# Activations, conditioning, states and small vectors handed over with channels on partitions, in the mLSTM + NSA decoder step

## The reference, cut to what matters

```python
def ada_norm(x, c, g, w_ada, b_ada):
    shift, scale, gate = jnp.split(c @ w_ada + b_ada, 3, axis=-1)
    h = rmsnorm(x, g) * (1 + scale[:, None, :]) + shift[:, None, :]
    return h, gate[:, None, :]

def mlstm_layer(x, c, C0, n0, m0, conv0, norm_g, ada_w, ada_b, w_in, gate_b, conv_w, conv_b, wq, wk, ...):
    h, gate = ada_norm(x, c, norm_g, ada_w, ada_b)
    proj = h @ w_in                     # xc, v, o, z and the gates ig, fg
    ...                                 # short convolution from conv0, q and k by 4x4 blocks wq, wk
    ...                                 # stabilised matrix memory from C0, n0, m0
    return x + gate * out, (C, n, m, new_conv)

def nsa_layer(x, c, ...):
    h, gate = ada_norm(x, c, norm_g, ada_w, ada_b)
    ...
    out = (o.astype(x.dtype) * jax.nn.silu(z)) @ w_out
    return x + gate * out               # y_prompt (1, 512, 1024) and y_sample (8, 4, 1024)
```

## Time and profile before

| what | value |
|---|---|
| median of 3 runs | 2076.85 us (2076.14 to 2081.01) |
| span of the profiled execution | 2075.2 us |
| PE busy | 1912.7 us, 92% of the span |
| DVE, ACT, POOL busy | 712.8, 473.6, 227.0 us |
| moved by DMA | 281.79 MB, mean 136 GB/s |

### The profile page before, as it was taken

One profiled execution on the slowest core, in us unless ns is written; L12 is line 12 of the kernel. 1 busy time (PEld: TensorE's weight loads), 2 busy tenths in 40 slices (PEclk: granted clock), 3 DMA queues, 4 the chain that ended last, 5 costly groups with the idle time before them and its releaser, 6 DMA issues. The chain is left out here.

```text
span 2075.2 us, 26135 instructions
## 1 busy us (share of the span) xinstructions
PE 1912.7 (92%) x9695; PEld 1154.3 (56%) x9695; DVE 712.8 (34%) x1620; ACT 473.6 (23%) x1032; POOL 227.0 (11%) x333
## 2 busy tenths in 40 slices
PE   5779999999999999997989999789889999999878
PEld 3345645564655565456864448655555555555467
DVE  3213232323242423240121314167652444444332
ACT  1311211211131112110011011246442333333310
POOL 0000100010001000100000000024352112111000
PEclk8879999999999999998999999779899999999989
DMA  9942561355135422635121236500024444443431
GB/s 299 387 155 72 201 215 43 120 180 187 43 143 183 162 80 106 229 116 219 41 81 41 81 59 245 169 26 2 1 79 186 177 179 173 182 178 123 138 88 43
DMA packets 119388, 281.79 MB, mean 136 GB/s; under 512 B 33320, under 2 KB 41966, under 8 KB 115543
## 3 DMA queue, kind: packets, MB, share of 16 engines
q1 hardware_dynamic: 101100, 170.57, 24.7%
q0 software_dynamic: 12928, 109.54, 13.2%
q10 hardware_dynamic: 5268, 0.36, 0.3%
HBM read 227.79 MB, written 60.86 MB: 139 GB/s over the span
## 5 line engine op out<-in xcount | busy, mean ns | idle before, releaser
L2187 PE MATMUL sample_bank<-area 128*128 128x508 f32 x512 | 234.3, 600 | 4.8 <-DVE area L2428 4.8
L1080 DVE SCALAR_TENSOR_TENSOR mlstm_cring<-mlstm_cring,mlstm_cur_old,mlstm_bank 128x512 f32<-128x512 f32 x128 | 87.1, 743 | 223.4 <-PE mlstm_bank L842 223.4
L2187 PEld LDWEIGHTS sample_bank<-area 128*128 128x128 f32 x512 | 92.0, 190 | 106.6 <-issue 98.7
L1368 PE MATMUL proj_bank<-stage,area 128*128 128x512 f32 x320 | 142.4, 603 | 6.3 <-ACT area L1445 6.3
L760 PE MATMUL mlstm_bank<-h,stage 128*128 128x272 f32 x512 | 126.7, 411 | 15.4 <-issue 10.9
L760 PEld LDWEIGHTS mlstm_bank<-h,stage 128*128 128x128 f32 x512 | 102.0, 200 | 39.3 <-issue 12.6
L815 PE MATMUL mlstm_bank<-h,stage 128*128 128x272 f32 x512 | 121.2, 395 | 0.0
L826 PE MATMUL mlstm_bank<-stage,h 128*128 128x512 f32 x256 | 114.1, 599 | 0.0
L815 PEld LDWEIGHTS mlstm_bank<-h,stage 128*128 128x128 f32 x512 | 96.0, 190 | 27.9 <-issue 9.1
L777 PE MATMUL mlstm_bank<-stage,h 128*128 128x512 f32 x256 | 110.9, 594 | 0.0
L1368 PEld LDWEIGHTS proj_bank<-stage,area 128*128 128x128 f32 x320 | 60.9, 193 | 87.5 <-issue 85.9
(11 more groups left out here) (513 smaller groups left out, 2709.1 us busy)
## 6 DMA issues: line engine op xcount, KB each, us to landing
stage<-in_a_w_in SPq DMA_DIRECT2D x16, 2048.0 KB, 8.9
mlstm_cring<-in_state_C SPq DMA_DIRECT2D x32, 1024.0 KB, 5.5
o_Cs<-mlstm_cring POOLq DMA_DIRECT2D x32, 1024.0 KB, 4.7
stage<-in_a_ada_w SPq DMA_DIRECT2D x4, 2048.0 KB, 12.6
sample_winr<-in_cache_kv_win SPq DMA_DIRECT2D x8, 1024.0 KB, 5.3
o_win_s<-in_cache_kv_win SPq DMA_DIRECT2D x1, 8128.0 KB
stage<-in_w_kv SPq DMA_DIRECT2D x3, 2048.0 KB, 7.7
act_scratch<-mlstm_szt POOLq DMA_DIRECT2D x4, 1088.0 KB, 8.3
```

Source lines behind the costliest of these rows:

```text
L1080: dve.scalar_tensor_tensor(c, c, cur_old[:, n:n + 1], bank[:, b_big("outer", n * KH + k), :], ALU.mult, ALU.add).then_inc(E["c_new"], 1)
L1368: last = pe.matmul(o, h[:, k, a * P:(a + 1) * P], w[:, k, :], start=(k == 0), stop=(k == KD - 1))
L2187: t = pe.matmul(out, S.w1[:, c, o * 8 + k, :], xt[:, k, :, o:o + M - 1], start=(k == 0 and o == 0), stop=(k == 7 and o == 1))
```

## The change

What arrives in HBM is laid out by the host: `x_t` (128 x 8 x 544, x of prompt and samples with channels on partitions), `first` (the turned conditioning, padded with zeros to 32 columns, and the gate weights, padded to 32), `vec` (the ten vectors with channels on partitions), `heads` (gate biases and `state_m`), `state` (`a_wq`, `a_wk`, the turned state of the convolution and the turned `n0`). 19 inputs go, 5 come. All transposes of L289 to L316 and the DVE copies of L467 to L481 go, and the spill with them; `phase_project` loads `x_t` in place of `S.x_scratch`. The output `y` leaves as 128 x 8 x 544 and the host turns it; each of the 8 blocks of `S.x1` is stored when it is ready.

```diff
@@ phase_inputs
-        x_nat = sb("x_nat", [P, TT, D])
-        xs_nat = sb("xs_nat", [SS, D])
-        c_nat = sb("c_nat", [NS + 1, D])
-        c_t = sb("c_t", [P, KD, SS])
-        rows1 = sb("rows1", [88, P])
-        rows2 = sb("rows2", [112, P])
-        conv_nat = sb("conv_nat", [NS * (CW - 1), AI])
+        first = sb("first", [P, 2, KD, SS])
+        c_t, gate_w = first[:, 0], first[:, 1]
...
@@ SP
             sp.dma_start(S.const1[:, :], I["const"][0:AH, S.n_late:]).then_inc(s_const, 16)
-            sp.dma_start(c_nat[0:1, :], I["c_prompt"]).then_inc(s_c, 16)
-            sp.dma_start(c_nat[1:, :], I["c_sample"]).then_inc(s_c, 16)
...
-            sp.dma_start(x_nat[:, :, :], I["x_prompt"].rearrange("o (a p) d -> p (o a) d", p=P)).then_inc(s_x, 16)
-            sp.dma_start(xs_nat[:, :], I["x_sample"].rearrange("n t d -> (n t) d")).then_inc(s_x, 16)
+            sp.dma_start(flat(first[:, :, :, :], "pgks"), I["first"]).then_inc(s_first, 16)
+            sp.dma_start(xt[:, :, :], I["x_t"]).then_inc(s_x, 16)
...
             for i in range(NCH):
-                if i == 2:
-                    sp.wait_ge(x_ok, KD + 1)
-                    sp.dma_start(S.x_scratch, xt[:, :, :]).then_inc(spill, 16)
                 if uses(i):
                     sp.wait_ge(ada_mm, earlier(i) + 1)
                 elif SLOT[i] == 2:
                     sp.wait_ge(sum_ok, 1)
                 elif SLOT[i] == 3:
-                    sp.wait_ge(spill, 16)
                     sp.wait_ge(x_used, 1)
@@ POOL
-            pool.memset(S.n0[0:1, :], 0.0)
-            pool.memset(m0[:, 0:1], 0.0)
-            pool.memset(gate_w[:, :, :], 0.0)
...
+            pool.memset(S.n0[0:1, :], 0.0).then_inc(zero_ok, 1)
@@ PE
             pe.wait_ge(s_const, 32)
-            pe.wait_ge(s_vec, 160)
...
+            pe.wait_ge(s_first, 16)
@@ ACT
-            act.dma_start(conv_nat[:, :], I["state_conv"].rearrange("o n j c -> (o n j) c")).then_inc(s_conv, 16)
...
+            act.dma_start(S.vec[:, :], I["vec"]).then_inc(s_vec, 16)
+            act.dma_start(heads[:, :], I["heads"]).then_inc(s_m0, 16)
+            act.dma_start(S.state[:, :], I["state"]).then_inc(s_state, 16)
+            act.dma_start(S.n0[1:, :], I["state_n"].rearrange("o n h d -> (o n) (h d)")).then_inc(s_state, 16)
+
+            act.wait_ge(s_x, 16)
             act.activation(sq[:, :, :], xt[:, :, :], ACT.Square).then_inc(sq_ok, 1)
@@ phase_project
-            sp.dma_start(S.x1[:, :, :], S.x_scratch).then_inc(E["x_in"], 16)
+            sp.dma_start(S.x1[:, :, :], I["x_t"]).then_inc(E["x_in"], 16)
@@ phase_output
-            for a in range(TT):
-                sp.wait_ge(E["y_ok"], 2 * a + 2)
-                sp.dma_start(I["o_yp"].rearrange("o (a p) d -> p (o a) d", p=P)[:, a, :], y[:, a, :]).then_inc(E["outs"], 16)
-            sp.wait_ge(E["y_ok"], 10)
-            sp.dma_start(I["o_ys"].rearrange("n t d -> (n t) d"), ys[:, :]).then_inc(E["outs"], 16)
-            sp.wait_ge(E["outs"], 16 * (TT + 1))
+            for m in range(KD):
+                sp.wait_ge(E["x_new"], m + 1)
+                sp.dma_start(I["o_y"][:, m, :], S.x1[:, m, :]).then_inc(E["outs"], 16)
+            sp.wait_ge(E["outs"], 16 * KD)
...
-            pe.wait_ge(E["x_new"], KD)
-
-            for a in range(TT + 1):
...
-                        last = pe.transpose(bank[0:rows, b, k * P:(k + 1) * P], S.x1[:, half * 4 + k, at:at + rows], ident)
-                    last.then_inc(E["tr"], 1)
...
-                dve.tensor_copy(dst, bank[0:rows, f % 8, :]).then_inc(E["y_ok"], 1)
```

More of the change, by code:

```diff
@@ L2585, in _ @@
                 last.then_inc(E["mm"], 1)
-            pe.wait_ge(E["x_new"], KD)
-            for a in range(TT + 1):
-                for half in range(2):
-                    f = 2 * a + half
-                    b = f % 8
-                    if f >= 8:
-                        pe.wait_ge(E["y_ok"], f - 7)
-                    rows, at = (P, a * P) if a < TT else (SS, TP)
-                    for k in range(4):
-                        last = pe.transpose(bank[0:rows, b, k * P:(k + 1) * P], S.x1[:, half * 4 + k, at:at + rows], ident)
-                    last.then_inc(E["tr"], 1)
         @block.vector
@@ L2704, in build, with small_layouts, turned @@
         phase_output(nc, I, S)
+def small_layouts(given):
+    def turned(a, rows):
+        return np.asarray(a).reshape(rows, -1, P).transpose(2, 1, 0)
+    x = np.concatenate([np.asarray(given["x_prompt"]).reshape(TP, D), np.asarray(given["x_sample"]).reshape(SS, D)], 0)
+    first = np.zeros((P, 2, KD, SS), np.float32)
+    first[:, 0, :, 0:1], first[:, 0, :, 1:NS + 1] = turned(given["c_prompt"], 1), turned(given["c_sample"], NS)
+    first[:, 1, :, 0:2 * AH] = np.asarray(given["a_w_in"])[0, :, 4 * AI:].reshape(KD, P, 2 * AH).transpose(1, 0, 2)
+    vec = np.concatenate([np.asarray(given[name]).reshape(-1, P) for name in (
+        "a_ada_b", "kv_ada_b", "b_ada_b", "a_norm_g", "kv_norm_g", "b_norm_g", "a_conv_w", "a_conv_b", "a_hnorm_g", "a_skip")], 0).T
+    heads = np.zeros((AH, 2 + NS + 1), np.float32)
+    heads[:, 0:2], heads[:, 3:] = np.asarray(given["a_gate_b"])[0].T, np.asarray(given["state_m"])[0].T
+    state = np.zeros((P, 656), np.float32)
+    for j, name in enumerate(("a_wq", "a_wk")):
+        state[:, 64 * j:64 * j + 64] = np.asarray(given[name])[0].reshape(16, P, 4).transpose(1, 0, 2).reshape(P, 64)
+    state[:, 128:512] = turned(given["state_conv"], NS * (CW - 1)).reshape(P, 16 * 24)
+    n0 = np.zeros((P, 16, NS + 1), np.float32)
+    n0[:, :, 1:] = turned(given["state_n"], NS)
+    state[:, 512:] = n0.reshape(P, 144)
+    return {"x_t": turned(x, T), "first": first.reshape(P, 2 * KD * SS), "vec": vec, "heads": heads, "state": state}
 def kernel(**inputs):
@@ L2712 @@
     arrays, I = {}, {}
-    for name, a in inputs.items():
+    given = {**inputs, **small_layouts(inputs)}
+    for name in ("x_prompt", "x_sample", "c_prompt", "c_sample", "a_ada_b", "kv_ada_b", "b_ada_b", "a_norm_g", "kv_norm_g", "b_norm_g", "a_conv_w",
+                 "a_conv_b", "a_hnorm_g", "a_skip", "a_gate_b", "state_m", "a_wq", "a_wk", "state_conv"):
+        del given[name]
+    for name, a in given.items():
         a = np.ascontiguousarray(a)
@@ L2723 @@
     r = run(nc, [arrays], core_ids=[0])
[L2724 removed]
+    got = r.results[0]
+    y = np.asarray(got["o_y"]).transpose(2, 1, 0).reshape(T, D)
+    return (y[None, :TP], y[TP:].reshape(NS, TS_, D), *(got[name] for name in OUTS if name != "o_y"))
```

112 lines of the change are left out of this document (18 added, 94 removed).

## The result

| kernel | median us (lowest to highest) | span of the profiled execution | ratio to before, 95% interval |
|---|---|---|---|
| before | 2078.88 (2076.14 to 2081.01) | 2075.2 | |
| changed | 2044.57 (2039.99 to 2046.06) | 2043.5 | 0.9837 [0.9816, 0.9857] |

Each kernel has four runs; three of the four before gave the median of 2076.85 from which the prediction started. The change is worth 34.3 us in the medians and 31.7 us between the two profiled executions. The prediction had 19.3. Both terms of its sum are there; a third one, larger than either, it didn't have.

The account below looks back on a forecast made before the run. The prediction took loads to bound the first phase and PE what follows; 12.5 us at the start plus 6.8 at the end gave 19.3 us, span 2055.9, median 2057.5 us, range 2053.5 to 2063.5.

Parts of the forecast that it names:

- Both terms of its sum: Start of the kernel 12.5 us earlier and end 6.8 us shorter, together 19.3 us.
- takes over a time that is saved ahead of it: After the first phase PE, 98% busy, is the bound, so time saved earlier reaches the kernel's end whole.
- what was to prove me wrong: A product behind chunk 2 waiting on something besides DMA, a changed stream rate, or PE's later busy time growing.
- x's landing: First phase: x lands at 12.6 us, after 3.80 MB of loads; bounds 11.5 and 16.84.
- The chain behind it: After x: square 3.83, signal 0.1, sums 3.64, chunk 0's products 2.9; chunk 2 issued at 23.2, 12.5 us earlier.
- Moves as one: The stream stays unbroken, so everything behind chunk 2 shifts together and the whole 12.5 us arrive at 139.64.
- the tail of 18.7 us: End of the first phase, from chunk 14's products to the next phase's first product: PE empties its list, alike in both kernels.
- the slower rival: Inputs leave HBM, so the `ada` weights lie elsewhere and are read more slowly: 2094.0 us at 272 GB/s; chance 0.03.
- the hole: First phase, before the stream of chunk loads: 0 GB/s from 34 to 36 us; expected to remain some 2 us.
- the cap: All first-phase loads, 41.5 MB, without a break end at 110.2: 14.4 us gained there, 2055.6 us in all; chance 0.10.
- cost no more than the hole beside which they ran: First phase: the spill's 2.2 MB add no separate gain when removed; they are in the 12.5 us.
- The end: Output phase: without the last transposes and copies, stores by block save 6.8 us; lower bound 6.0.

Follow-up runs that it names:

- the changed kernel's second profile: The changed kernel run again with no edit: 2045.9 us, ratio 0.9858.
- four kernels: The kernel before (2078.88 us) and the changed kernel with 150, 168 and 184 empty PE instructions ahead of the first product (2053.55, 2066.99, 2072.51 us).

## Why the prediction was wrong

**The step that failed** is the one it opens with: PE "takes over a time that is saved ahead of it", and from 139.64 on everything was to move as one. That holds only if the code behind runs as before, and PE's instructions moved, too: the change's first part took 168 of them out ahead of a loop, and was costed by what they did on the path, not by the room they took. The missing term is 17.6 to 18.3 us in the positions and 10.4 to 13.4 in the medians, against 11.3 for the start. The rows were there to be read: the "issue" of 10.9 us at L760, and the fetches of instructions. The windows, with PE 98% busy, looked like a PE that lacks nothing; a product that takes 0.35 us at 0.63 of the clock, in place of 0.25, counts as busy, too. No rival named a gain behind the first phase, and what was to prove me wrong was that PE's busy time there grew; it fell, by 1.8 to 3.0 us in each of passes 2 to 4.

**x's landing** was mis-sized: 12.6 foretold, the square started at 14.31. The first 4 us (117 GB/s) and the rate behind them (five windows, 0.393 MB/us on average, against 0.39) were right. The amount wasn't: by 14.0 us 4 x 0.117 + 2 x (0.382 + 0.407 + 0.428 + 0.395 + 0.354) = 4.40 MB had moved, not the 3.80 that are issued ahead of x and with it. 0.6 MB more, 1.5 us, passed x while it was still in flight; behind it in SP's queue stand only the chunks.

**The chain behind it** held: square 3.83, hand-over 0.14, sums 3.64. The products of chunk 0 took 2.46 us, between the bounds of 2.21 and 3.64; I had taken 2.9. The clock rose during them, after PE had been at work since 18.28, as it had before from 28.04; where PE stood still just ahead of them, with x ahead of the constants, they took 3.64. (That the clock is released by activity, as the Trainium skill has it in "TensorE: Matmul & The Clock Gate", "What's actually happening", agrees; that the turning's removal would keep it down through these products does not.) So they end at 24.36 and not 23.1, and the gain is 11.3 us in place of 12.5: x came 1.7 us later than foretold, and the products took 0.4 less.

**"Moves as one", inside the first phase,** was right: 11.34 us at chunk 2's products, 11.30 at chunks 14 and 15, 11.18 at the loop's first product. The last agreement has luck in it: the tail of 18.7 us was to be alike in both kernels, and the two profiled executions had it so (18.8 in the changed one), but the changed kernel's second profile took 20.5 and has the loop's first product 10.5 us ahead of the old place. The rate of the stream stayed, so the slower rival had nothing; the hole stayed, so the cap wasn't reached, and the run with x ahead of the constants shows that an earlier x didn't remove it (64 GB/s from 24 to 26 us), since chunk 0's own landing comes next. Chunk 5's issue, at 34.94, lies well inside the stream.

**The spill** "cost no more than the hole beside which they ran". For the kernel before that reading may stand, but in the changed one the spill, put back, costs chunk 2 2.7 us and chunk 14 2.1, so its removal is a part of the 11.3 and not nothing. In the medians that doesn't show.

**The end** was right: 7.0 us of positions (the block ready at 2040.23, the span's end 3.3 later, against 10.3), foretold 6.8. From the last issue to the end it took 3.2 us where I took 3.46, so the store of twice the size costs no more. The estimate of 2.6 us by the Trainium skill ("DMA: Bandwidth & Descriptors", "Anatomy of one DMA") is still shorter than the 3.2 here; the page gives that fit for DMAs on GpSimd's path, though, and this store is issued by SP.

**The sum**: 11.2 + 7.1 = 18.3 us, against 19.3, as far as it went. With the loop's 18.3 and the 4.9 that later phases gave back in that execution it is 31.7.

## What to carry to other kernels

An edit that takes instructions out ahead of a loop moves the loop's start within the blocks of 16 KB in which PE's code is fetched. In this loop, at some places the blocks are fetched anew in every pass, and where too little work then lies between the jump's target and its block's end, each pass pays: up to 5.4 us of idle time and a lower clock behind it, nothing at the best places. So look for idle time that ends by "issue" at the first instructions of a loop, count the instructions that an edit takes away or adds ahead of it, and before giving a small gain or loss to the edit itself, put the loop back with empty instructions and time that. A load's landing is to be counted with a part of what is issued behind it, not only with what is ahead.

## What the runs showed of the hardware that I had not expected

- Behind a jump back over the loop of 1647 instructions, with 1146 to 1210 instructions ahead of it, PE's code is fetched anew, 9 blocks in each of passes 2 to 4. The target's own block comes first, and the loop's first product starts 1.67 to 1.78 us after it has landed. The next block's fetch starts 6.3 to 7.0 us after the first's, so PE stops at the end of the target's block until 5.96 to 6.59 us after the loop's first product (12 jumps, four kernels). With 35 products ahead of that end there is no such stall. With 1026 to 1066 instructions ahead of the loop (1254 and 1282 in the kernel before) that queue fetches nothing in passes 2 to 4.
- After a stall of 3.25 us the granted clock of the next 7.8 us is 0.63, which costs another 2.2 us.
- About 100 empty instructions (two waits of the code each) ahead of the first product were free, hidden by x's landing; the further ones took 0.1 us each.
- PE waits 1.8 and 2.8 us longer for two transfers in later phases with 88 empty instructions than without, in phases whose lines are alike; why isn't known.
